# Feed-forward end with the last gated block turned inside the row products before it, and the residual by column halves

## The reference, cut to what matters

```python
# first block, per layer: feed-forward, token mixer, feed-forward; each
h = rms_norm(x, g_pre) * (1 + scale) + shift
y = swiglu(h) or token_mixer(h)          # swiglu: (silu(h @ w_gate) * (h @ w_up)) @ w_down, 2816 wide
x = x + res_w * (1 + gate) * rms_norm(y, g_post)
# second block, per layer: attention, then 16 experts of which each token takes 2; each
h = rms_norm(x, g) * (1 + scale) + shift
x = x + gate * (attention(h) or grouped_moe(h))
```

## Time and profile before

| | us |
|---|---|
| median of 3 runs | 2297.01 (2294.2 to 2298.27) |
| the profiled execution | 2283.29 |
| its span | 2281.3 |
| TensorE busy | 2049.3 (90%) |
| VectorE busy | 1438.7 (63%) |
| ScalarE busy | 848.0 (37%) |
| GpSimd busy | 67.6 (3%) |

### The profile page before, as it was taken

One profiled execution on the slowest core, in us unless ns is written; L12 is line 12 of the kernel. 1 busy time (PEld: TensorE's weight loads), 2 busy tenths in 40 slices (PEclk: granted clock), 3 DMA queues, 4 the chain that ended last, 5 costly groups with the idle time before them and its releaser, 6 DMA issues.

```text
span 2281.3 us, 26827 instructions
## 1 busy us (share of the span) xinstructions
PE 2049.3 (90%) x9772; PEld 1513.4 (66%) x9772; DVE 1438.7 (63%) x2212; ACT 848.0 (37%) x1037; POOL 67.6 (3%) x93
## 2 busy tenths in 40 slices
PE   2999899988999899899988999886899879879997
PEld 2778788866887688778876788665544337654442
DVE  6888676656887888776656898676511137652111
ACT  3333545544343434554564433542200025321000
POOL 0000000000000000000000000110000001000000
PEclk9999999999999999999998999987999989999999
DMA  8999344334887699444432898341599985239997
GB/s 343 383 361 379 134 172 141 136 110 189 332 356 304 253 357 372 185 176 150 141 116 98 331 375 356 136 143 62 209 415 422 421 331 200 104 131 418 421 421 304
DMA packets 86332, 592.53 MB, mean 260 GB/s; under 512 B 9680, under 2 KB 13136, under 8 KB 15568
## 3 DMA queue, kind: packets, MB, share of 16 engines
q1 hardware_dynamic: 79760, 579.90, 64.3%
q10 hardware_dynamic: 6464, 11.15, 1.5%
HBM read 589.96 MB, written 1.05 MB: 259 GB/s over the span
## 4 chain that ended last, share of the span: by engine, by line
PE 71%; DMA 11%; DVE 10%; ACT 4%; issue 2%; POOL 1%; SPq 0%; ACTq 0%; DVEq 0%; POOLq 0%
PE acc L1828 12%; PE acc L1832 11%; PE acc L1831 11%; PE gu L2130 8%; PE gu L1828 6%; PE gu L1832 6%; PE gu L1831 6%; DMA w_raw<-wstream 5%; PE tr L2130 4%; DMA stage<-wstream 3%; PE acc L2130 3%; PE tr L1892 3%; DVE w_lo L1048 2%; DMA proj<-ada_stream 2%; DVE tf L1687 1%
## 5 line engine op out<-in xcount | busy, mean ns | idle before, releaser
L1048 DVE TENSOR_TENSOR w_lo<-stage,w_hi 128x2048 fp32r<-128x2048 f32 x240 | 547.6, 2286 | 68.0 <-ACT w_hi L578 67.9
L578 ACT ACTIVATE w_hi<-stage 128x2048 fp32r<-128x2048 f32 x240 | 457.4, 1911 | 279.1 <-PE acc L1832 261.3
L1120 DVE SCALAR_TENSOR_TENSOR proj<-proj,c_row 128x1024 f32<-128x1024 f32 x240 | 291.5, 1218 | 53.4 <-DMA proj<-ada_stream 44.7
L1828 PE MATMUL acc<-w_hi,hT_hi 128*128 128x512 f32 (+1 forms) x736 | 308.6, 419 | 5.1 <-DVE hT_lo L1392 5.1
L1828 PE MATMUL gu<-w_hi,hT_hi 128*128 128x512 f32 x704 | 283.8, 403 | 11.1 <-DVE pair L1189 10.8
L1831 PE MATMUL acc<-w_lo,hT_hi 128*128 128x512 f32 (+1 forms) x736 | 292.0, 397 | 0.0
L1832 PE MATMUL acc<-w_hi,hT_lo 128*128 128x512 f32 (+1 forms) x736 | 291.9, 397 | 0.0
L1832 PE MATMUL gu<-w_hi,hT_lo 128*128 128x512 f32 x704 | 277.7, 394 | 0.0
L1831 PE MATMUL gu<-w_lo,hT_hi 128*128 128x512 f32 x704 | 277.5, 394 | 0.0
L1828 PE MATMUL acc<-w_hi,yT_hi 128*128 128x512 f32 (+1 forms) x460 | 183.8, 400 | 14.0 <-DVE yT_lo L1604 5.7
L2130 PE MATMUL gu<-stage,got 128*64 128x512 f32 x768 | 170.6, 594 | 15.0 <-DMA stage<-wstream 15.0
(11 more groups left out here) (221 smaller groups left out, 2449.0 us busy)
## 6 DMA issues: line engine op xcount, KB each, us to landing
stage<-wstream SPq DMA_DIRECT2D x336, 1024.0 KB, 5.3
proj<-ada_stream SPq DMA_DIRECT2D x120, 1024.0 KB, 7.7
w_raw<-wstream SPq DMA_DIRECT2D x96, 1024.0 KB, 18.0
tf<-bgate_in ACTq DMA_DIRECT2D x12, 256.0 KB, 4.3
proj<-rel_in ACTq DMA_DIRECT2D x16, 192.0 KB, 2.3
proj<-t_in ACTq DMA_DIRECT2D x8, 192.0 KB, 3.4
z_mix<-c_in ACTq DMA_DIRECT2D x2, 512.0 KB, 7.7
x_tok<-x_in ACTq DMA_DIRECT2D x1, 1024.0 KB, 19.8
```

Of the source, the lines that this page charges most:

```text
L578: act.activation(w_hi[:, n % PARTS, :], stage[:, n % STAGES, :], ACT.Copy).then_inc(hi_ready, 1)
L1048: dve.tensor_tensor(w_lo[:, n % PARTS, :], stage[:, n % STAGES, :], w_hi[:, n % PARTS, :].bitcast(F32), ALU.subtract).then_inc(chunk_ready, 1)
L1120: ins = dve.scalar_tensor_tensor(w, w, 1.0, c_row[:], ALU.mult, ALU.mult, accum_out=dst)
L1828: ins = pe.matmul(dst, l_hi, r_hi, start=start, stop=False, skip_group_check=True)
```

## The change

- **Feed-forward end, TensorE.** The loop over blocks runs one double turn less and blocks 9 and 10 are written out. The rows of block 9 are cut: its first 6 of 24 products, then the turn of block 10, then the other 18, then the 24 of block 10. Block 10 has buffers of its own (`end_hi`, `end_lo`). ScalarE and VectorE convert the last chunk ahead of the gated block 10 instead of behind it.
- **Residual and squares by column halves.** Each 1024-wide square is two 512-wide ones (GpSimd adds the two sums), each product and each addition of the residual is two. The first product of a half waits for `acc_read` (the first square is done), the first square of x for `x_part`. Ahead of the addition of t = 1, VectorE waits for the root of the next norm's t = 0 (`rs_done`).
- **Join behind the first expert layer.** The next chunk's high part moves behind `y_high`, its low part to just ahead of the norm's first `scaled`.
- **Expert ring.** Chunks 12 and 13 of each expert layer get two buffers used once (`once`, over `z_mix` and `prob`), and can be loaded as soon as the step before is over.
- **Start.** SyncE begins with the chunks one slice later (m = 7). The low part of chunk 0 comes behind the first `scaled`, the high part of chunk 1 behind the first high part of h.

```diff
@@ sync
-                if m >= NORM_SLICES - 2 and n < 8:
+                if m >= NORM_SLICES - 1 and n < 8:
                     chunk(n)
...
-                if not isinstance(i, int) or n - n0 >= RING:
+                if not isinstance(i, int) or n - n0 >= RING + ONCE:
                     sp.wait_ge(chunk_ready, n + 1 - RING + RING * i)
@@ gpsimd
+                pool.tensor_scalar(ss[:, at:at + 1], ss[:, at:at + 1], ss[:, at + 8:at + 9], EPS, ALU.add,
+                                   ALU.add).then_inc(pool_up, 1)
@@ scalar
+                for h in range(2):
+                    if parts:
+                        act.wait_ge(x_ready if h else x_part, parts)
+                    ins = act.activation(both[:, h, :], halves[h], ACT.Square, scale=D ** -0.5,
+                                         accum_out=ss[:, at + 8 * h:at + 8 * h + 1])
+                    if h == 0 and read is not None:
+                        ins.then_inc(read, 1)
+                ins.then_inc(rs_req, 1)
...
-                silu(nb - 1)
                 hi(n0 + 3 * nb - 1)
-                turn_hi(nb - 1, hidden_turn(b["u"], nb - 1))
+                silu(nb - 1)
+                act.wait_ge(tr_full, hidden_turn(b["u"], nb - 1) + 1)
+                act.wait_ge(pe_used, n0 + 1 + PARTS)
+                act.activation(end_hi, tr[:, hidden_turn(b["u"], nb - 1) % 2, :], ACT.Copy).then_inc(th_ready, 1)
...
-                    if p == PAIRS - 1 and end < n_chunks:
-                        act.wait_ge(chunk_ready, moe_up_at(n0, p, 1, 1, 1) + 1)
-                        hi(end)
                     y_high(p, 0)
                     y_high(p, 1)
+                act.wait_ge(chunk_ready, end)
+                ahead(end)
@@ vector
-                if m == NORM_SLICES - 1:
-                    lo(0)
...
-                    if p == PAIRS - 1:
-                        dve.wait_ge(chunk_ready, moe_up_at(n0, p, 1, 1, 1) + 1)
-                        ahead(end)
...
+            def residual(k, b, t, after=None, between=None):
+                gated, row = tok[:, 1 - t, :], x[:, t, :]
+                for h in range(2):
+                    c = slice(512 * h, 512 * h + 512)
+                    if k < 6:
+                        dve.wait_ge(rs_req, resid_request(b, t)) if h else dve.wait_ge(acc_read, NT * k + t + 1)
...
+                    dve.tensor_tensor(gated[:, c], acc[:, 2 * t + h, :], tok[:, 0, c], ALU.mult).then_inc(dve_up, 1)
...
+                if k < 6:
+                    dve.wait_ge(rs_done, resid_request(b, t))
+                if after:
+                    dve.wait_ge(rs_done, norm_request(after, k + 1, 0))
+                for h in range(2):
+                    c = slice(512 * h, 512 * h + 512)
+                    dve.wait_ge(dve_up, ups - 1 + h)
...
+                    ins.then_inc(x_ready if h else x_part, 1)
...
+                    if k == 3 * DEPTH + 2:
+                        dve.wait_ge(chunk_ready, b["n"])
+                        lo(b["n"])
                     scaled(0)
+                    if k == 0:
+                        lo(0)
@@ tensor
-                turn_hidden(nb - 1)
-                down(n0 + 3 * nb - 1, nb - 1, False, True)
+                g = nb - 1
+                block_(g - 1)
+                up(n0 + 3 * g - 1, 0, g)
+                turn_hidden(g - 1)
+                up(n0 + 3 * g, 1, g)
...
+                row_part(prev, 0, (0,), of(hid_hi, hid_lo), False)
+                turn_hidden(g)
+                row_part(prev, 0, (1,), of(hid_hi, hid_lo), False)
+                row_part(prev, 1, (0, 1), of(hid_hi, hid_lo), False).then_inc(pe_used, 1)
+                pe.wait_ge(tr_free, hidden_turn(b["u"], g) + 1 + 2)
+                chunk_wait(last)
+                row_part(last, 0, (0, 1), of(end_hi, end_lo), True).then_inc(half_done, 1)
+                row_part(last, 1, (0, 1), of(end_hi, end_lo), True).then_inc(pe_used, 1)
```

More of the change, by code:

```diff
@@ L256, in staging_slots @@
 def staging_slots(plan):
-    used, slots = [0] * RING, []
+    used, slots = [0] * (RING + ONCE), []
     first = [b["n"] for step, b in plan if step[0] == "ffn" and step[3]]
@@ L261, in staging_slots @@
         c = [n - n0 for n0 in first if 0 <= n - n0 < 3 * MOE_BLOCKS]
-        slot = c[0] % RING if c and c[0] % RING >= STAGES else n % STAGES
+        slot = n % STAGES
+        if c and RING <= c[0] < RING + ONCE:
+            slot = c[0]
+        elif c and c[0] % RING >= STAGES:
+            slot = c[0] % RING
         slots.append((slot, used[slot]))
@@ L377, in build @@
         h_banks = [acc[:, j, :] for j in range(4)] + [gu[:, j, :] for j in range(2)]
-        landed = [sem(f"landed{i}") for i in range(RING)]
+        landed = [sem(f"landed{i}") for i in range(RING + ONCE)]
         chunk_ready = sem("chunk_ready")
@@ L448, in moe_tile @@
         def moe_tile(n, n0):
+            if RING <= n - n0 < RING + ONCE:
+                return once[n - n0 - RING]
             e = (n - n0) % RING - STAGES
@@ L526, in _ @@
                 stream(n, n0)
-                for c in range(RING):
+                for c in range(2 * RING):
                     expert_chunk(n0 + c, n0)
-                with sp.Fori(0, PAIRS - 1) as i:
+                with sp.Fori(0, PAIRS - 2) as i:
                     for c in range(RING):
-                        expert_chunk(n0 + RING + c, n0, i)
+                        expert_chunk(n0 + 2 * RING + c, n0, i)
                 n = n0 + 3 * MOE_BLOCKS
@@ L553, in root, with row_root @@
                 pool.tensor_tensor(rs[:, c], ss[:, c], mhalf[:, c], ALU.pow).then_inc(rs_done, 1)
-            for step, b in plan:
-                kind = step[0]
-                if kind == "norm" or (kind == "resid" and step[1] < 6):
-                    for t in range(NT):
-                        root(b, 1, t + (NT if kind == "resid" else 0), t)
+            def row_root(request, at):
+                nonlocal ups
+                pool.wait_ge(rs_req, request)
+                pool.tensor_scalar(ss[:, at:at + 1], ss[:, at:at + 1], ss[:, at + 8:at + 9], EPS, ALU.add,
+                                   ALU.add).then_inc(pool_up, 1)
+                ups += 1
+                pool.wait_ge(pool_up, ups)
+                pool.tensor_tensor(rs[:, at:at + 1], ss[:, at:at + 1], mhalf[:, at:at + 1], ALU.pow).then_inc(rs_done, 1)
+            for at, (step, b) in enumerate(plan):
+                kind = step[0]
+                if kind == "norm":
+                    row_root(norm_request(b, step[1], 0), 0)
+                    row_root(norm_request(b, step[1], 1), 1)
+                elif kind == "resid" and step[1] < 6:
+                    row_root(resid_request(b, 0), NT)
+                    row_root(resid_request(b, 1), NT + 1)
                 elif kind == "mixer":
@@ L610, in squares, with mean_square, row_halves, gated_square @@
                 ins.then_inc(rs_req, 1)
-            def mean_square(b, t, src, at):
-                if b["req"] + t:
-                    act.wait_ge(rs_req, b["req"] + t)
-                act.activation(pair[:].rearrange("p a t c -> p (a t c)"), src, ACT.Square, scale=D ** -0.5,
-                               accum_out=ss[:, at:at + 1]).then_inc(rs_req, 1)
+            def mean_square(request, at, halves, parts=None, read=None):
+                if request > 1:
+                    act.wait_ge(rs_req, request - 1)
+                for h in range(2):
[6 more added lines that the diff above has]
+                ins.then_inc(rs_req, 1)
+            def row_halves(t):
+                return [x[:, t, 512 * h:512 * h + 512] for h in range(2)]
+            def gated_square(b, k, t):
+                act.wait_ge(pe_used, b["n"] + PARTS) if t else act.wait_ge(half_done, k + 1)
+                mean_square(resid_request(b, t), NT + t, [acc[:, 2 * t + h, :] for h in range(2)], read=acc_read)
             def take_hi(b, rounds, dst, plain, width=512):
@@ L967, in _ @@
             for t in range(NT):
-                mean_square(plan[0][1], t, x[:, t, :], t)
+                mean_square(norm_request(plan[0][1], 0, t), t, row_halves(t))
             for t in range(NT):
-                by_root(plan[0][1], t)
-            ahead(0)
+                by_root(plan[0][1], 0, t)
+            hi(0)
             for step, b in plan:
@@ L1255, in moe @@
                 u0 = b["u"]
-                end = n0 + 3 * MOE_BLOCKS
                 def take(what, dst):
@@ L1866, in columns, with row_part @@
                 ins.then_inc(pe_used, 1)
+            def row_part(n, t, ks, lhs, last):
+                s = n % PARTS
+                for k in ks:
+                    l_hi, l_lo = lhs(k, t)
+                    for h in range(2):
+                        c = slice(k * D + h * 512, k * D + (h + 1) * 512)
+                        ins = mm3(acc[:, 2 * t + h, :], l_hi, l_lo, w_hi[:, s, c], w_lo[:, s, c], False, last and k == 1)
+                return ins
             def rows(n, lhs, first, last, i=0, rounds=1):
```

(5 more changed lines are left out.)

86 lines of the change are left out of this document (48 added, 38 removed).

## The result

| | before | changed |
|---|---|---|
| median on the same chip | 2295.61 us (2294.12 to 2298.27) | 2279.43 us (2276.76 to 2280.77) |
| ratio | | 0.9932 [0.9917, 0.9947] |
| the profiled execution | 2283.29 us, clock 0.966 | 2276.76 us, clock 0.964 |
| GpSimd busy | 67.6 us | 62.7 us |

The changed kernel is faster by 16.2 us at the median, where I had forecast 7.9. Most local steps can be read in the trace. A ratio is the changed time over the time of before, with its 95% interval.

A forecast was written before the change was run, and what follows sets the result against it. TensorE was taken as the bound almost everywhere, DMA in the first slices and expert layers. Terms -4.8 - 2.1 - 2.5 - 2.8 + 0 + 0.1 + 4.2 gave -7.9 us, 2289.1 on the median 2297.01; range 2280 to 2297.

The forecast's parts named there:

- Feed-forward end: End of each feed-forward: wait for the last turned block's low part goes, new 0.2 us wait comes; -1.2 four times, -4.8.
- Join behind the first expert layer: After the first expert layer: result made before the next chunk's conversions, so `scaled` comes near 1867.3; -2.8 us.
- Start: Kernel start: early gain of 3.9 us lost because chunk 4 lands late, then a slice 4.2 later; +4.2 us.
- expert layer's end: End of the first expert layer, without the join's own halves: 3.5 less 1.7, about 1.8 us faster.
- end of the kernel: Last passes of the kernel: eight 512-wide passes in place of four 1024-wide ones; +0.1 us.
- The two buffers used once: Both expert layers: earlier loads only lengthen the DMA queue's dry stretch before chunk 20; 0 us.
- Rival B: Expert layers: buffers used once pay, 5.0 us less to load in each of two layers; 2279 us, chance 7%.
- Joins: First block's six joins: scaled x 0.35 us earlier each, -2.1; two joins behind the attentions: -1.25 each, -2.5.
- Rival C: Joins and feed-forward end: halves give nothing, half the feed-forward gain is lost; -0.9 us, 2296.1, chance 15%.
- Rival D: Nine joins: DVE's new wait on the norm's root lands on the path; +6.6 us, 2303.6, chance 8%.
- Rival A: Kernel start: chunk 4 on time, so the start keeps its gain; -16 to -12 us, about 2283, chance 20%.

The follow-up runs named there:

- the repetition: The changed kernel run again, unchanged: 2277.99 us against 2292.86 for the kernel before, ratio 0.9935.

## Why the prediction was wrong

Forecast at the median -7.9, measured -16.2 and, repeated, -15. By ratio at 2293 us:

| part | forecast | measured |
|---|---|---|
| feed-forward end | -4.8 | -4.1 alone |
| joins, with the one behind the first expert layer | -5.6 | -7.1 alone |
| expert layer's end | -1.8 | 0.5 alone, -4.0 in company |
| buffers used once | 0 | -4.6 alone, -2 to -4 in company |
| end of the kernel | +0.1 | not separated |
| start | +4.2 | +4.8 alone |

With the -4.0, and the others as measured alone, the column sums to -15.0. Each value is uncertain by 2 to 4 us, so the sum proves only that nothing large is missing. (The join behind the expert layer is one term in the prediction, -2.8; here its 0.95 for the root stands with the joins.)

- **The two buffers used once** is the step that failed: "I cost it at nothing", because the DMA queue was dry by chunk 20 and "from chunk 20 on the transfers follow one another as before". Both were wrong. I read the dry queue from half a microsecond of 197 GB/s; chunk 19 was still on its way in it, and landed 3.6 us after chunk 20 was issued. With the buffers chunk 20 lands 4.8 us after its issue and not 6.7 to 7.0, and one wait of TensorE for a raw chunk goes in each layer: 1.0 to 1.5 of the 5.0 us reach the first layer, about 1 the second. What else the profiles show of this part lies in the attention between the layers, at a higher clock with the first layer's buffers, which I had not thought of. Rival B named the buffers and, with 2279, the measured time, but that is luck: it wanted 5 us from each layer.
- **Join behind the first expert layer.** The wait was right: `scaled` came 3.3 us earlier by the clock of the trace, 3.8 counted from the root ahead of the layer, of which some 1.1 is the buffers': -2.7 for a forecast of -2.8. Two things I did not see. The second half of the tokens comes later: TensorE's wait for it is 3.12, 1.89 before. And with the old end TensorE is at the lower clock ahead of the join, with the new one at the higher. Taken out of the changed kernel the new end costs 4.0, where I had 1.8. And it doesn't pay alone: behind the whole addition the power takes 2.46 and the gain is gone.
- **Joins.** 0.45 per join for 0.35 forecast (4.97 to 4.52; 5.27 to 4.52 behind the third feed-forward), from another split: the halves cost next to nothing on the path (5.03 without the hold, 4.97 whole) and the hold gives 0.5, not 0.81. Behind the first attention TensorE's wait for scaled x fell from 3.77 to 2.58, behind the second from 3.77 to 2.94: -1.2 and -0.8 for -1.25 each; behind the first the wait for the second half of the tokens rose from 1.88 to 2.38 (2.12 in the repetition) and takes some of it back. Rival C fell: the power is 0.56 to 0.57 at each norm's t = 0. Rival D fell where it weighed most, as the wait for the second half, 1.88 in the feed-forward joins before, is 1.88 still; but the hold does cost 0.8 us behind the expert layer and 0.35 behind the second attention.
- **Feed-forward end.** Right, to the new wait of 0.21.
- **Start.** Right in place and mechanism, and near enough in size (3.0 us at the slice, 3.3 in company, 4.8 alone, for 4.2): 8.22 us to land, 63.84, 96.28. The figure of the Trainium skill that the prediction set beside its 8.29 us is from a section on DMAs issued by GpSimd, and SyncE issues these; the section that speaks of every DMA (SBUF — State Buffer, The DMA setup-cost knee) has about the same, so that 6.8 us stands as its estimate, and the 8.22 does not agree with it. Rival A is what happens when chunk 4 is issued ahead of the wait: then the early gain stays (235.9).
- **The base.** I added a sum made on the profiled execution to the median. That was no error in itself, but the profiled execution of before was one that none of 81 runs reaches in clock, and so the near match of the profiles (-6.5) would have hidden the error. The medians carry a clock of 0.959 before and 0.962 after. 0.003 of TensorE's 2050 busy us is 6 us, which is an upper estimate of what the clock adds, since a slower TensorE hides elsewhere at times.

Open: why the joins alone come with a higher mean clock, why the attention's clock goes with the buffers of the layer ahead, and where 3 of the 5 us of the held addition lie.

## What to carry to other kernels

A wait in front of an issuing queue is paid by whatever stands behind it: count the chunks ahead of each wait before moving a loop bound by one; here one chunk was worth 8 us. A change that pays nothing alone may pay in company, when a piece of the other part removes a collision that it brings; test it both ways, and test which piece, as here it was the halves and not the hold. Before you call a DMA queue dry, look at when the transfer ahead landed, not at the bandwidth of a moment. A single profile is one draw of the clock: compare its granted clock with that of the timed runs before you set a sum on it.

## What the runs showed that I had not expected

- GpSimd's power on 128 x 1 took 0.56 us alone, 0.84 to 1.5 beside an addition of two SBUF operands on VectorE and 2.46 beside a 128 x 2048 subtraction, each time ending some 0.4 us after VectorE's operation did.
- The clock loss of feed-forward stages two to four was 3.4 or 5.1 us in every profile, nothing between, and that of a mixer stage from 5.1 to 11.9, these two in two profiles of the same kernel (before). 81 runs of one kernel spread over 16 us.
